# Squares in PSUM, tanh in place of Silu and sigmoid, and a reordered merging of branches in a kernel of two transformer blocks

## The reference, cut to what matters

```python
# first block: three mixers side by side on h = norm(x) * (1 + sc) + sh; proj = h @ w_in
q_b = silu(b_q) * 64 ** -0.5                                # HGRN2
k_b = (1 - lb) * sigmoid(-z)                                # per direction, z = forget columns
la_b = log_sigmoid(z) + log1p(lb * exp(min(-z, 80)))
o_b = rms_norm(bidir_scan(q_b, k_b, v_b, la_b), g) * silu(b_g)
o_c = rms_norm(bidir_scan(q_c, k_c, v_c, la_c), g) * silu(c_g)       # GLA
o_a = rms_norm(differential_attention(...), g)              # two softmax maps, 4 heads
g_a, g_b, g_c = sigmoid(gates)                              # 3 x 1024 columns
merged = g_a * (o_a @ w_up_a) + g_b * (o_b @ w_up_b) + g_c * (o_c @ w_up_c)
x = x + gt_m * (merged @ w_out)
x = x + gt_f * (square(relu(h2 @ mlp_w1)) @ mlp_w2)         # h2: norm of x, scaled and shifted
return rms_norm(x)
# second block: attention, conv-gated FFN, chunked SGU, conv-gated FFN, each as
x = x + rms_norm(f(rms_norm(x, pre)), post)
```

## Time and profile before

| | before |
|---|---|
| median of the runs | 2381.29 us (2379.55 to 2382.61) |
| the profiled execution, its own time | 2383.91 us |
| its span in the profile | 2382.2 us |
| TensorE, matmuls | busy 2285.8 us, 96% |
| TensorE, weight loads | busy 1905.5 us, 80% |
| VectorE | busy 1143.4 us, 48% |
| ScalarE | busy 1016.9 us, 43% |
| GpSimd | busy 1053.1 us, 44% |
| moved by DMA | 239.8 MB, 101 GB/s on average |

### The profile page before, as it was taken

How to read it: one execution, slowest core, us unless ns; L and a number is a source line. 1 busy time by engine, 2 the same in 40 slices (tenths; PEclk the granted TensorE clock), 3 DMA queues, 4 the chain that set the end, 5 groups by cost and what they waited for, 6 DMA issues and landing times. The chain is left out here.

```text
span 2382.2 us, 28986 instructions
## 1 busy us (share of the span) xinstructions
PE 2285.8 (96%) x11624; PEld 1905.5 (80%) x11624; DVE 1143.4 (48%) x1746; ACT 1016.9 (43%) x1897; POOL 1053.1 (44%) x804
## 2 busy tenths in 40 slices
PE   7989988999999999999999999999999999999998
PEld 4768766777888888888888888878888888888887
DVE  3666877755441122457475244451343345724253
ACT  4675566644443232555553222363332235422224
POOL 1444333343544454632435444534444443544454
PEclk9989999999999999999999999999999999999999
DMA  7221232356222322321212222323222222222321
GB/s 280 80 71 71 107 120 93 133 177 239 89 80 97 106 89 91 109 76 36 89 54 106 89 90 105 106 71 106 89 89 89 90 87 72 95 100 86 109 90 70
DMA packets 42663, 239.80 MB, mean 101 GB/s; under 512 B 5024, under 2 KB 7072, under 8 KB 17184
## 3 DMA queue, kind: packets, MB, share of 16 engines
q1 hardware_dynamic: 39328, 231.23, 27.2%
q10 hardware_dynamic: 3200, 6.71, 1.0%
HBM read 226.38 MB, written 8.39 MB: 99 GB/s over the span
## 5 line engine op out<-in xcount | busy, mean ns | idle before, releaser
L2571 POOL TENSOR_TENSOR WL<-RAW,WH 128x512 fp32r<-128x512 f32 (+1 forms) x692 | 913.5, 1349 | 1173.3 <-ACT WH L1277 1162.0
L723 PE MATMUL PS<-HHI,WH 128*128 128x512 f32 x1496 | 601.3, 402 | 2.2 <-DVE HLO L1855 1.6
L723 PE MATMUL PS<-HHI,WL 128*128 128x512 f32 x1496 | 585.8, 392 | 0.0
L723 PE MATMUL PS<-HLO,WH 128*128 128x512 f32 x1496 | 585.6, 391 | 0.0
L1277 ACT ACTIVATE WH<-RAW 128x512 fp32r<-128x512 f32 (+1 forms) x692 | 379.9, 612 | 403.7 <-PE PS L723 382.3
L723 PEld LDWEIGHTS PS<-HHI,WH 128*128 128x128 f32 x1496 | 283.0, 189 | 75.8 <-issue 13.8
L723 PEld LDWEIGHTS PS<-HHI,WL 128*128 128x128 f32 x1496 | 282.5, 189 | 60.7
L723 PEld LDWEIGHTS PS<-HLO,WH 128*128 128x128 f32 x1496 | 283.3, 189 | 57.2 <-issue 2.2
L723 PE MATMUL PS<-UF,WH 128*128 128x512 f32 (+1 forms) x832 | 225.7, 359 | 0.0
L1855 DVE TENSOR_TENSOR T<-PS,R 128x512 f32<-128x512 f32 x112 | 76.9, 690 | 212.4 <-PE PS L723 204.4
L723 PEld LDWEIGHTS PS<-UF,WH 128*128 128x128 f32 x832 | 149.8, 191 | 22.8
(11 more groups left out here) (352 smaller groups left out, 3611.1 us busy)
## 6 DMA issues: line engine op xcount, KB each, us to landing
RAW<-in_wts SPq DMA_DIRECT2D x190, 1024.0 KB, 4.8
FW<-in_wts SPq DMA_DIRECT2D x6, 1024.0 KB, 17.3
spill<-T SPq DMA_DIRECT2D x24, 256.0 KB, 3.3
RAW<-in_wts SPq DMA_DIRECT2D x8, 768.0 KB, 4.1
GT<-spill SPq DMA_DIRECT2D x20, 256.0 KB, 4.8
X<-in_xt SPq DMA_DIRECT2D x2, 1024.0 KB, 9.2
out_x<-X SPq DMA_DIRECT2D x8, 256.0 KB, 2.2
X<-in_xt SPq DMA_DIRECT2D x2, 768.0 KB, 9.4
```

Source lines behind the costliest of these rows:

```text
L723: return e.matmul(o_, l, r, start=start, stop=stop)
L2571: return e.tensor_tensor(o_, a, b, f)
```

## The change

1. Rows: the decays' steps start at 16 and 34 with distances 2 and 2.2 (before: 19 and 30, both 1.5). They are nine in place of seven: the two scans of the backward decay are in steps of their own (6 and 7), the scaling of the keys is step 8.
2. Mixers: Silu is computed as tanh(x/2) on ScalarE and (t + 1) * x by one VectorE instruction, which reads x from PSUM. The factor of a half is in the scale for `bq` (0.0625) and in the root's exponent for `cg` and `bg`. The sigmoid into `K_` becomes one VectorE instruction (max(z, 0) plus the logarithm at hand) and an exponential, in step 1 of `decay`'s ScalarE part. Copies are issued a row later.
3. Banks: the first `out` tile is in bank 3 and the ring has seven banks; the mean of branch a is in bank 0.
4. Merging: sigmoids are a unit ahead, high parts stand between, and each low part comes after the first product of the next column.
5. Stage ends: squares 1 to 3 of the first half and square 3 of the second go into PSUM bank 6. The additions of the first half are VectorE's, each right behind the next take. On ScalarE the last square of the first half stands ahead of the split of b; two quarters of b follow it, the others come at columns 1 and 2. GpSimd makes all quarters of a and b, then its two additions.

```diff
 NATURAL = ("cv", "bv", "av")
-GATE_C, DECAY, RECUR, ATTEND = (1, 2), ((19, 1.5), (30, 1.5)), (9, 1.1), (75, 1.7)
+GATE_C, DECAY, RECUR, ATTEND = (1, 2), ((16, 2), (34, 2.2)), (9, 1.1), (75, 1.7)
...
     def decays(self, p):
-        for n in range(7):
+        for n in range(9):
             yield [("decay", p, n)]
...
-        self.take(six, *[(at["out", j], m) for j in range(2) for m in range(4)])
+        self.take([3, 4, 5, 6, 0, 1, 2], *[(at["out", j], m) for j in range(2) for m in range(4)])
...
                     step = [("nat", i, m, row // 2)] * (row % 2 == 0) if natural else [("gemm", i, m, 2 * row)]
-                    yield step + beside[r] + (late if row == 1 else [])
+                    yield step + beside[r] + (late if row == 1 else []) + (later if row == 2 else []) + (copies if row == 3 else [])
                 late = [("evict", i, tag, n, m)]
+                later = [("silu", i, tag, m)] if tag in ("cg", "bg", "bq") else []
+                copies = [("copies", m)] if tag == "bq" else []
...
         if kind == "a":
-            return 2, 1, 128, ones, SC[:, 3:4], None, (OA[:, n, 0, :], OA[:, n, 1, :]), T0[1][:, :], SS[:, :]
+            return 2, 0, 128, ones, SC[:, 3:4], None, (OA[:, n, 0, :], OA[:, n, 1, :]), T0[1][:, :], SS[:, :]
...
-    def square_of(p):
-        return SS if p == 0 else SQ if p == 2 else T0[0]
+    def square_of(hf, p):
+        return SS[:, :] if p == 0 else PS[:, 6, :] if hf == 0 or p == 3 else SQ[:, :] if p == 2 else T0[0][:, :]
...
                     q.wait_ge(*at(("sum", n, 0)))
-                elif p == 2 and hf:
-                    q.wait_ge(*at(("ssa", n, 0, 2)))
-                elif p == 3:
-                    q.wait_ge(*at(("ssa", n, hf, 1)))
-                elif p == 1 and hf:
-                    q.wait_ge(*at(("ssa", n, 0, 3)))
-                dst = square_of(p)[:, :].rearrange("p (k t) -> p k t", k=2)
+                elif p > 1 and hf == 0:
+                    q.wait_ge(*at(("ssa", n, 0, p - 1)))
+                dst = square_of(hf, p).rearrange("p (k t) -> p k t", k=2)
...
             squares(0, 2)
-            for p in range(4):
-                split(b, p)
             table()
             squares(0, 3)
+            for p in range(2):
+                split(b, p)
...
                 high(0, k)
-                if 4 + k < 5:
-                    split(b, 4 + k - 1)
+                if k < 3:
+                    split(b, 1 + k)
...
             TA, TB, TC = [g_[:, :, :] for g_ in G3]
-            if n == 0:
+            if n == 1:
                 q.wait_ge(*at(("ev", U["bz", p], 1)))
-                e.activation(K_, Z, ACT.Sigmoid, scale=-1.0).then_inc(*up("a_mix", ("sg", p)))
-            elif n == 1:
...
                 e.activation(TC, TC, ACT.Exp, scale=-1.0).then_inc(*up("a_mix", ("ec", p)))
+                q.wait_ge(*at(("lk", p)))
+                e.activation(K_, K_, ACT.Exp, scale=-1.0).then_inc(*up("a_mix", ("sg", p)))
...
                 q.wait_ge(*at(("t", i, m)))
-            if tag == "cg":
-                e.activation(GC[:, m, :], ps, ACT.Silu).then_inc(*up("a_ev", ("ev", i, m)))
+            if tag in ("cg", "bg"):
+                e.activation((GC if tag == "cg" else GB)[:, m, :], ps, ACT.Tanh, scale=0.5).then_inc(*up("a_ev", ("tanh", i, m)))
             elif tag == "bq":
                 tm = T0[2 + m]
                 q.wait_ge(*at(("h", "mix", 6 + m)))
-                e.activation(tm[:, :], ps, ACT.Silu).then_inc(*up("a_ev", ("ev", i, m)))
-                q.wait_ge(*at(("q_scaled", m)))
-                for k in range(4):
-                    h2, d = k // 2, k % 2
-                    t = e.dma_start(keyed(2 * m + h2)[64 * d:64 * d + 64, 0, :], tm[64 * h2:64 * h2 + 64, :])
-                    t.then_inc(*up(f"dupq{m}", *([("qb", m)] if k == 3 else []), by=16))
-            elif tag == "bg":
-                e.activation(GB[:, m, :], ps, ACT.Silu).then_inc(*up("a_ev", ("ev", i, m)))
+                e.activation(tm[:, :], ps, ACT.Tanh, scale=0.5).then_inc(*up("a_ev", ("tanh", i, m)))
...
+        def copies(m):
+            q.wait_ge(*at(("q_scaled", m)))
+            for k in range(4):
+                h2, d = k // 2, k % 2
+                t = e.dma_start(keyed(2 * m + h2)[64 * d:64 * d + 64, 0, :], T0[2 + m][64 * h2:64 * h2 + 64, :])
+                t.then_inc(*up(f"dupq{m}", *([("qb", m)] if k == 3 else []), by=16))
...
-        for j in range(4):
-            i = U["up", j]
-            split_after(i)
+        def sigmoids(j):
             for s in range(6):
...
                 e.activation(G, G, ACT.Sigmoid).then_inc(*up("a_ev", ("sig", j, s)))
...
+        def merged_high(k):
+            q.wait_ge(*at(("gsum", k)))
+            for kind, n in boxes:
+                q.wait_ge(*at(("o", kind, n)))
+            e.activation(ME[:, k, 0, :], GT[k // 2 % 3][k % 2][:, :], ACT.Copy).then_inc(*up("h_hi", ("merged_hi", k)))
+        sigmoids(0)
+        for j in range(4):
+            split_after(U["up", j])
+            merged_high(2 * j)
+            if j < 3:
+                sigmoids(j + 1)
+            merged_high(2 * j + 1)
...
                 take(0, p)
+                if p > 1:
+                    add(0, p - 1)
...
         def decay(p, n):
-            Z = ZB[:, 2 * p:2 * p + 2, :]
+            Z, K_ = ZB[:, 2 * p:2 * p + 2, :], QKB[:, 2 - 2 * p:4 - 2 * p, 1, :]
             TA, TB, TC = [g_[:, :, :] for g_ in G3]
...
-            elif n == 2:
+            if n == 2:
...
                 q.wait_ge(*at(("la", p)))
+                stt(K_, Z, 0.0, TA, MAX, ADD).then_inc(*up("d_mix", ("lk", p)))
+                q.wait_ge(*at(("lk", p)))
...
                 q.wait_ge(*at(("log_b", p)))
-                scans(ZB, (2 * p, 2 * p + 1), "decay_b")
+                scans(ZB, (2 * p,), "decay_b")
+            elif n == 7:
+                q.wait_ge(*at(("log_b", p)))
+                scans(ZB, (2 * p + 1,), "decay_b")
+            elif n == 8:
+                q.wait_ge(*at(("sg", p)))
+                q.wait_ge(*at(("lb", 5)))
+                for h in (2 * p, 2 * p + 1):
+                    ts(keyed(h)[:, 1, :], keyed(h)[:, 1, :], LB[:, 16 + h:17 + h], None, MUL).then_inc(*up("d_mix", ("kb", h)))
...
                 e.tensor_copy(VC[:, 2 * m:2 * m + 2, :], ps.rearrange("p (t n) -> p t n", t=2)).then_inc(*up("d_ev", ("ev", i, m), ("vc", m)))
-            elif tag == "bq":
-                q.wait_ge(*at(("ev", i, m)))
-                ts(T0[2 + m][:, :], T0[2 + m][:, :], 0.125, None, MUL).then_inc(*up("d_mix", ("q_scaled", m)))
...
+        def silu(i, tag, m):
+            a = T0[2 + m][:, :] if tag == "bq" else (GC if tag == "cg" else GB)[:, m, :]
+            q.wait_ge(*at(("tanh", i, m)))
+            stt(a, a, 1.0, PS[:, BANK[i, m], :], ADD, MUL).then_inc(*up("d_ev", ("ev", i, m)))
+            if tag == "bq":
+                q.wait_ge(*at(("ev", i, m)))
+                ts(a, a, 0.0625, None, MUL).then_inc(*up("d_mix", ("q_scaled", m)))
...
         stt(AF[:, :], MOD[:, 32:40], 1.0, v("gmlp", 0, 8), ADD, MUL).then_inc(*up("d_mix", ("af",)))
-        for j in range(4):
+        def merged_low(k):
+            q.wait_ge(*at(("merged_hi", k)))
+            t = tt(ME[:, k, 1, :], GT[k // 2 % 3][k % 2][:, :], ME[:, k, 0, :].bitcast(F32), SUB)
+            t.then_inc(*up("h_lo_d", ("merged", k), ("gt_free", k // 2, k % 2)))
+        for k in range(8):
+            j, m = k // 2, k % 2
             i = U["up", j]
...
+            G = [GT[j % 3][2 * g + m][:, :] for g in range(3)]
+            for g in range(3):
+                q.wait_ge(*at(("t", i, m, g)))
+                q.wait_ge(*at(("sig", j, 2 * g + m)))
+                tt(G[g], PS[:, BANK[i, m, g], :], G[g], MUL).then_inc(*up("d_ev", ("ev", i, m, g)))
+                if g == 0 and k:
+                    merged_low(k - 1)
...
+        merged_low(7)
...
+            def add(p):
+                q.wait_ge(*at(("sqp", n, 1, p)))
+                q.wait_ge(*at(("ssa", n, 1, p - 1) if p > 1 else ("sqp", n, 1, 0)))
+                tt(SS[:, :], SS[:, :], square_of(1, p), ADD).then_inc(*up("p_norm", ("ssa", n, 1, p)))
             for p in range(4):
                 split(t1, p)
             if nx is None:
-                add(0, 1)
-                add(0, 2)
...
                 return
-            split(a, 0)
-            split(a, 1)
-            add(0, 1)
-            split(a, 2)
-            split(a, 3)
-            add(0, 2)
-            for p in range(4):
-                split(b, p)
-            add(1, 1)
-            for p in range(4, 4):
-                split(b, p)
-            add(1, 2)
+            for u in (a, b):
+                for p in range(4):
+                    split(u, p)
+            add(1)
+            add(2)
```

More of the change, by code:

```diff
@@ L1 @@
+import math
 import concourse.bass as bass
@@ L331, in projections @@
     def projections(self):
-        late = []
+        late, later, copies = [], [], []
         for tag, n in DENSE:
@@ L446, in build @@
```

(41 more changed lines are left out.)

15 lines of the change are left out of this document (4 added, 11 removed).

## The result

The changed kernel takes 2346.72 us, the median of four runs (2339.93 to 2348.02), beside 2381.77 us of the kernel before (four runs, 2379.55 to 2382.61). The ratio is 0.9849, with a 95% interval of 0.9828 to 0.9869: 35 us faster. The forecast was 2341 us with a range of 2328 to 2364. The time is in the range and also in the likeliest case's own (2330 to 2352). The gain is 6 us smaller than the forecast's 41.

The account below looks back on a forecast made before the run. TensorE, busy 2285.8 of 2382.2 us, was taken as the bound, so only its waits and the slow clock behind them count. Stage ends 24.9, merging 7.2, mixers 3.8 and 5.1 sum to 41.0 us: 2341 us, range 2328 to 2364.

Parts of the forecast that it names:

- The stage ends: Four stage ends: TensorE's waits for the sum of squares go, 16.3 us, plus 10.6 of clock, less 2.0; net 24.9.
- what is late next: Following layer's columns behind the stage ends: TensorE waits 0.4 to 1.6 us at each, 2.0 in all, between 0 and 8.
- The merging: Before the output projection: the 5.13 us wait and 2.35 of clock go, less 0.3 for early sigmoids; net 7.2 us.
- the new ring: Output projection: first four tiles get banks 3 to 6, so TensorE's 5.13 us wait for bank 0 goes.
- The mixers: Mixers: earlier ScalarE and VectorE work shortens TensorE's waits; early part 5.1 us, late part 3.8.
- Silu on ScalarE: Mixers: replacing Silu by tanh removes table loads; 4.3 us in the early part and 3.3 in the late part.
- The bank: Late mixers: the mean in bank 0 frees TensorE from the logarithm; 0.5 us for two waits, about 0.7 for work left.
- a table of its own: Rival, mixers: each tanh costs 2.57 us as Silu did; 2349, or 2355 us with extra VectorE work; chance 0.08.
- The gain is eaten at the columns: Rival: stage ends lose 8 to 10 us at columns, added VectorE work another 5 to 9; say 2356 us; chance 0.20.
- The mixers unlock: Rival: chained mixer waits, 19.0 and 11.1 us, nearly all go with half their clock; 2325 us; chance 0.11.
- The slower case: Rival, mixers: the second decay's later scans make TensorE wait some 1.2 us per further row; 2390 us; chance 0.03.
- the signs of being right: Stage-end SS waits under 0.5 us, additions near 0.69, clock 1.00; no first-output-tile wait; 12 fewer loads; 4.87 us wait split.

Follow-up runs that it names:

- run 10: The changed kernel with ScalarE's new order at the stage ends, but squares in SBUF and GpSimd's additions as before: 2351.69 us, ratio 0.9886.
- run 9: The changed kernel with ScalarE's order at the stage ends as before, the squares still in PSUM: 2348.95 us, ratio 0.9879.
- second profile: Trace of the slowest run (2350.30 us) when the changed kernel was run again with no edit; median 2347.16 us, ratio 0.9866.
- run 8: The changed kernel with GpSimd's first addition of the second half ahead of the third quarter of unit b: 2344.55 us, ratio 0.9857.
- run 11: The changed kernel with the out tiles' old ring (bank 0 first), the merging's new order kept: 2345.58 us, ratio 0.9861.
- run 6: The changed kernel with the decays as before (sigmoid on ScalarE, both scans in one step, rows 19 and 30): 2351.02 us, ratio 0.9883.
- run 5: The changed kernel with Silu back on ScalarE in place of tanh, copies a row earlier again: 2359.40 us, ratio 0.9905.
- run 12: The changed kernel with GpSimd's first addition moved ahead of b's third quarter, plus each decay scan one step later: 2342.03 us, ratio 0.9842.

## Why the prediction was right, and where it was not

**The stage ends: the mechanism right, one term too small.** The wait was wholly removed as summed: 16.4 us of idle time over four ends, and the clock is 1.00 behind all four. An addition of two SBUF inputs took 3.98, 1.01, 2.57 and 3.86 us beside GpSimd's low parts in the kernel before and 0.69 in the five other cases, which together make the mean of 1653 ns in the earlier trace rows. In run 10 it takes 2.89, 1.82 and 1.81 us where low parts overlap nearly all of it, and 0.69 at the first end, where one overlaps it by 0.5 us. One with a PSUM input beside the same work takes 0.69 in run 9. The Trainium skill ("GPSIMD Engine Reference", "1. Specifications") says that GpSimd shares its SBUF interfaces with VectorE and contends with VectorE instructions that have two SBUF inputs; these rows agree.

The time by which a matmul of the second profile is ahead of the same matmul of before shows the rest (us):

| stage end | at the sum of the first half | highest behind it | behind the next columns |
|---|---|---|---|
| 1 | 20.05 | 22.74 | 21.30 |
| 2 | 24.76 | 26.30 | 24.58 |
| 3 | 29.19 | 31.81 | 30.31 |
| 4 | 32.96 | 35.77 | 34.06 |

The clock gave 2.7 + 1.5 + 2.6 + 2.8 = 9.7 us, where the prediction had 10.6. The columns took back 1.4 + 1.7 + 1.5 + 1.7 = 6.4 us, 4.3 of them as longer waits for HLO. This is the step that was mis-sized, "what is late next": 2.0 us, between 0 and 8. Its cause was in part another too. The prediction expected a TensorE at full clock to overtake the columns' chain, and VectorE to stand at GpSimd's addition. The stand is there, 1.25 us at each end. But run 9 has the full clock and no later columns than before, so it is the new order of ScalarE that makes them late: through that stand, and through GpSimd's low parts, which stretch the HLO instructions beside them. The second was not in the prediction's sum. How the 6.4 us divide between the two is not measured beyond run 8's 2.8. A further 1.6 us is noise between executions: a clock fall at some 1706 us behind a wait of 1.8 us that was there before too. So 16.4 + 9.7 - 6.4 - 1.6 = 18.1 of the 18.2 us.

By the timed runs the stage ends alone give 13.3 us (8.6 to 15.9), further below 24.9 than any pair of traces; why the timed runs give less isn't shown, beyond that the profile of before is of a run of 2383.91 us, near its slowest.

**The merging: right in size, not in its cause.** 6.1 and 6.3 us where 7.2 were forecast. The text gave the new ring as the reason and the order as help; run 11 shows that the order alone does it. Whether the ring alone would have done it too is not shown.

**The mixers: right in the sum only, and that by luck.** 9.2 us in the second profile against 8.9, and by halves (a matmul at 251.02 us before, 244.96 after) 6.1 and 3.2 against 5.1 and 3.8. But the division among causes isn't confirmed. Silu on ScalarE costs 10.4 us in the changed kernel, of which 8.0 early, where the text had 4.3; in run 6 the decays' part is worth 5.2 early (a matmul at 250.20 in run 6, 244.96 in the changed kernel); their sum is far more than the 6.1 gained, so they overlap. With the change's decays alone (run 5) that matmul is at 252.92, with its tanh alone (run 6) at 250.20, against 251.02 before: each by itself is worth next to nothing there, both together 6.1. The bank, put at some 1 us in all, is worth nothing measurable. The count of table loads was right: 39 between 60 and 600 us before, 27 after, twelve fewer. The lines of tanh are L1630 for `cg` and `bg`, which has no load, and L1634 for `bq`, which has one for its two tiles (ScalarE's groups of the changed kernel, 60 to 600 us):

```profile
L1634 ACT ACT_TABLE_LOAD x1 | 1.3, 1283 | 0.0
```

So tanh doesn't need a table of its own beside the exponential here, as the Trainium skill ("ScalarE: Activation LUTs", "Table sets: the hidden batching unit") lists it, and that rival falls.

**The rivals.** "The gain is eaten at the columns" had the right direction: the columns cost 6.4 us, where it asked for 8 to 10. But no clock fell there, and VectorE's queue in the mixers did not add to it: the waits for SCT are 15.9 and 16.2 us in the two profiles, 19.0 before. "The mixers unlock" asked for 16 us more than the 8.9 of the sum; the profile with the most has 17.6 in all at the first `up` matmul, 8.7 more. The slower case did not show. Of the signs of being right all came: the wait of 4.87 us too was split into two smaller ones, 1.45 and 0.71 us in the second profile.

**Sum.** By the second profile 9.2 + 6.3 + 18.2 = 33.8 us, against 8.9 + 7.2 + 24.9 = 41.0. The wait at 127 us is 1.99 or 2.13 us long in two profiles of kernels with the change's mixers and 3.46 to 3.49 in seven others. In the two the clock over the 13 us behind the wait at 109 us is 0.74, in all seven 0.87, and TensorE takes 15.8 and 14.3 us between the two waits. What stays open is why the clock falls for longer in the two behind waits of nearly the same length (2.31 and 2.39 us; 2.26 to 2.30).

## What to carry to other kernels

When work is moved out of the way of one chain, price what it will stand beside in its new place. Here two quarters of a weight unit no longer stood in front of the last square and held up the next layer's columns instead, at a cost of some 6 us beside a gain of 26. At first it looks as if a faster TensorE had overtaken its suppliers; the run with the old order and the same clock told the two apart. A wait of 3 to 5 us cost its length and some six tenths as much again in clock (16.4 and 9.7 us). Shortening these waits by either means was worth most of the gain, and the second means for the same wait added little. Before a gain is read off two traces, find the same instruction in both and check how far executions of one kernel lie apart.

## What was not expected of the hardware

Two waits of equal length do not leave the same clock behind. In front of a matmul on `US` (the SGU) TensorE waits 1.81 us in both profiles of the changed kernel; in the first it goes on at full clock, in the second at 0.72:

```profile
1706.86 0.73 PE L727 MATMUL PS<-US,WH 128*128 128x512 f32 x2 [1.81 <-DVE T L1865]
```

```profile
1706.00:1712.00 6.00, 5.14 (x16) 4.07 (x17) 3.62 (x6) 3.34 (x6) 2.95 (x3) 0.72 0.53 178
```

For `KH` it waited 2.94 us in the changed kernel's first profile and in run 12's, and went on at 1.00 and at 0.77. At the stage ends waits of 2.53 and 2.80 us (runs 9 and 10) left full clock and those of 2.62 (run 9) and 2.78 (before) 0.72 over the next 6 us. Of the waits at 127 us those of 1.25 to 2.13 us left 1.00 behind and those of 3.46 to 3.49 us 0.74. This is part of why the executions of one kernel lie some 10 us apart. And a longer fall can pay for itself in part: the one at 109 us made TensorE late enough to meet VectorE with a shorter wait and no second fall.
